# Low halves of a split-precision kernel's weights placed 64 bytes further in SBUF

## What is computed

```python
for l in range(DEPTH):                                   # DEPTH = 1
    x = x + 0.5 * swiglu(rms_norm(x, ffn1_norm[l]), ffn1_gate[l], ffn1_up[l], ffn1_down[l])
    x = x + hybrid_mixer(rms_norm(x, mix_norm[l]), w_in[l], ..., w_out[l], lam_init)
    x = x + 0.5 * swiglu(rms_norm(x, ffn2_norm[l]), ffn2_gate[l], ffn2_up[l], ffn2_down[l])
return rms_norm(x, final_norm)

def swiglu(h, w_gate, w_up, w_down):                     # D_FF = 2816
    return (jax.nn.silu(h @ w_gate) * (h @ w_up)) @ w_down
```

## The kernel before

| tiles | start modulo 256 |
|---|---|
| xg_hi, xg_lo, w_hi, w_lo, h_hi_s, h_hi_w, h_lo, mixed_hi, mixed_lo, first_hi, first_lo | 128 |
| s_hi, s_lo (behind `offset_of_s`, 192 bytes), raw_u, t_raw | 64 |
| sum_hi, sum_lo (behind `offset_of_sums`, 64 bytes), gate_s, snap, sq | 128 |
| x, raw, rinv, ones | 0 |

## Time and profile before

### The profile page before, as it was taken

One profiled execution on the slowest core, in us unless ns is written; L12 is line 12 of the kernel. 1 busy time (PEld: TensorE's weight loads), 2 busy tenths in 40 slices (PEclk: granted clock), 3 DMA queues, 4 the chain that ended last, 5 costly groups with the idle time before them and its releaser, 6 DMA issues. The chain is left out here.

```text
span 990.8 us, 16666 instructions
## 1 busy us (share of the span) xinstructions
PE 964.2 (97%) x6360; PEld 859.3 (87%) x6360; DVE 682.7 (69%) x945; ACT 438.7 (44%) x688; POOL 355.9 (36%) x232
## 2 busy tenths in 40 slices
PE   9999999999999999999989999999999999999996
PEld 8789999998888888777978788888999999888885
DVE  6599998997534364775756874459999998753344
ACT  7555455545422223555723233354555555543331
POOL 0767767670012151000102004377776767000002
PEclk9999999999999999999989999999999999999998
DMA  6323333322232244112211113233333232222222
GB/s 203 119 95 103 109 112 100 117 95 83 94 93 96 95 131 136 65 47 66 74 39 65 64 65 107 85 107 106 114 99 124 88 127 85 85 92 79 97 95 86
DMA packets 30638, 95.07 MB, mean 96 GB/s; under 512 B 4112, under 2 KB 7344, under 8 KB 30592
## 3 DMA queue, kind: packets, MB, share of 16 engines
q1 hardware_dynamic: 28400, 90.98, 28.4%
q0 software_dynamic: 896, 2.39, 0.9%
q10 hardware_dynamic: 1296, 1.07, 0.3%
HBM read 92.00 MB, written 2.42 MB: 95 GB/s over the span
## 5 line engine op out<-in xcount | busy, mean ns | idle before, releaser
L1376 DVE TENSOR_TENSOR w_lo<-raw,w_hi 128x1024 fp32r<-128x1024 f32 (+3 forms) x130 | 187.2, 1440 | 167.4 <-ACT w_hi L1002 167.3
L1002 ACT ACTIVATE w_hi<-raw 128x1024 fp32r<-128x1024 f32 (+3 forms) x130 | 134.2, 1032 | 208.8 <-PE ps L508 208.8
L506 PE MATMUL ps<-xg_hi,w_hi 128*128 128x256 f32 (+1 forms) x552 | 188.1, 341 | 4.1 <-DVE w_lo L1376 2.5
L508 PE MATMUL ps<-xg_hi,w_lo 128*128 128x256 f32 (+1 forms) x552 | 184.4, 334 | 0.0
L507 PE MATMUL ps<-xg_lo,w_hi 128*128 128x256 f32 (+1 forms) x552 | 184.2, 334 | 0.0
L506 PE MATMUL ps<-s_hi,sum_hi 128*128 128x256 f32 x576 | 159.8, 277 | 2.2 <-ACT snap L1095 2.1
L507 PE MATMUL ps<-s_lo,sum_hi 128*128 128x256 f32 x576 | 159.3, 277 | 0.0
L508 PE MATMUL ps<-s_hi,sum_lo 128*128 128x256 f32 x576 | 159.2, 276 | 0.0
L507 PE MATMUL ps<-h_lo,w_hi 128*128 128x512 f32 x330 | 128.4, 389 | 0.0
L506 PEld LDWEIGHTS ps<-xg_hi,w_hi 128*128 128x128 f32 x552 | 104.3, 189 | 24.1 <-issue 13.5
L508 PEld LDWEIGHTS ps<-xg_hi,w_lo 128*128 128x128 f32 x552 | 104.4, 189 | 10.9
(11 more groups left out here) (240 smaller groups left out, 1906.8 us busy)
## 6 DMA issues: line engine op xcount, KB each, us to landing
raw<-up_w SPq DMA_DIRECT2D x50, 512.0 KB, 4.2
raw<-down_w SPq DMA_DIRECT2D x38, 512.0 KB, 3.3
raw_u<-up_w SPq DMA_DIRECT2D x36, 512.0 KB, 3.4
raw<-t_w SPq DMA_DIRECT2D x18, 512.0 KB, 3.3
raw<-out_w SPq DMA_DIRECT2D x8, 512.0 KB, 3.3
raw<-nat_w SPq DMA_DIRECT2D x6, 576.0 KB, 3.9
x<-xT SPq DMA_DIRECT2D x8, 256.0 KB, 6.0
out<-x SPq DMA_DIRECT2D x8, 256.0 KB, 2.2
```

What stands on the lines that cost most here:

```text
L506: pe.matmul(out_ap, a[0], b[0], start=first, stop=False, skip_group_check=resumed)
L508: return pe.matmul(out_ap, a[1], b[0], start=False, stop=last, skip_group_check=resumed)
L1002: act.activation(dst, raw[:, slot(s), 0:w], ACT.Copy).then_inc(hi_ready, 1)
L1376: dve.tensor_tensor(lo, raw[:, slot(s), 0:w], hi, ALU.subtract).then_inc(lo_ready, 1)
```

## The change

Three unused tiles are added. One of 16 floats (64 bytes) ahead of `w_lo` moves it from 128 to 192 modulo 256, and one of 48 floats (192 bytes) behind it brings everything that follows back to its place modulo 256. One of 64 bytes ahead of `sum_lo` moves that from 128 to 192. No instruction, wait or transfer is added, removed or put elsewhere in the order.

```diff
@@ -162,7 +162,9 @@
         xg_hi = sb("xg_hi", [P, KT, S], F32R)
         xg_lo = sb("xg_lo", [P, KT, S], F32R)
         w_hi = sb("w_hi", [P, 2, SLOTW], F32R)
+        sb("below_w_lo", [P, 16])
         w_lo = sb("w_lo", [P, 2, SLOTW], F32R)
+        sb("above_w_lo", [P, 48])
 
 
         with ExitStack() as st:
@@ -174,6 +176,7 @@
             t_raw = sb("t_raw", [P, 3, HW], stack=st)
             sb("offset_of_sums", [P, 16], stack=st)
             sum_hi = sb("sum_hi", [P, 5, HW], F32R, stack=st)
+            sb("below_sum_lo", [P, 16], stack=st)
             sum_lo = sb("sum_lo", [P, 5, HW], F32R, stack=st)
             gate_s = sb("gate_s", [P, 2, S], stack=st)
             snap = sb("snap", [P, 3, HALF], stack=st)
```

## The result

The changed kernel takes 1004.04 us (median of 4 runs, 1003.03 to 1004.91) beside 993.21 us for the kernel before: a ratio of 1.0104, with a 95% interval of 1.0091 to 1.0117. It is slower by 1.0%, 10.8 us between the medians. The profiled span grew from 990.8 to 1003.0 us, by 12.2 us. One execution of the first kernel of experiment 7 (1589.72 us) and one of the kernel before beside it (1925.14 us) were slow and are left out of all medians and ratios.

A forecast was written before the change was run, and what follows sets the result against it. TensorE, busy 97% of the span, bounds the kernel by how closely matmuls follow. Gains of 4.4 + 2.9 = 7.3 us, less 0.8 us lost at waits, take 6.5 us off 992.66: 986.2 us; range 982.5 to 1001.5 us.

The forecast's parts named there:

- The constant belongs to the pair of addresses, not to the width.: TensorE matmuls: the remainder over the column rate, some 13 ns at distance 0, 6.6 ns for s, holds at every width.
- (a): 512-column matmuls with w_lo stationary: 658 steps go to distance 64, 6.7 ns less each, 4.4 us gained.
- A step depends on its own pair alone: Three-matmul products: only the step L507 to L508 gets a new distance and so a new time; 512 columns at 0.220 us.
- (b): 256 columns of xg under w_lo and sum_lo: 432 steps gain 6.7 ns each, 2.9 us.
- (c): sum_lo under s: 576 steps go from distance 64 to 128; bounds 3.8 us gain or loss, taken as nothing.
- (d): Token-major products: 96 steps stream w_lo under a load of xg_lo; bounds plus and minus 0.6 us, taken as nothing.
- (e): gate_s, snap and sq behind sum_lo move by 64 too; no cost, as VectorE has 8% in hand.
- (f): Everything behind w_lo moves by 256 bytes, none modulo 256, and no transfer changes in size: nothing.
- Broken locks: Rival, chance 0.28: after each jump TensorE's two streams never settle; 8.4 us more, 1001 us; 1009 us at full loss.
- Narrow only: Rival, chance 0.14: the 512-column step is already undisturbed, so its gain falls away; 2.9 us less, 990.1 us.
- Distance 128 collides: Rival, chance 0.10: sum_lo under s at distance 128 collides like 0, costing 3.8 us; 2.7 us less, 990.3 us.
- No effect: Rival, chance 0.12: addresses don't matter, s matmuls are faster for another reason; nothing moves, 992.9 us.

The follow-up runs named there:

- experiment 7: Against the kernel before: sum to 192, s to 128, w untouched, 1000.79 us; the same with unit slabs 16 floats further in their slots, 998.50 us.
- experiment 3: Against the kernel before: w and sum, both halves, at 192 and s at 128, so every loop has distance 64; 1006.38 us, ratio 1.0125.
- experiment 4: Against the kernel before, s kept at 64: w and sum, both halves, at 160, 192, 0, 64, 96; 1006.55, 1002.72, 1007.93, 1005.81, 1005.60 us, one run each.
- experiment 6: Against the kernel before: xg, w and mixed, both halves, all at 192; h, s and sum keep their places modulo 256; 1003.27 us, one run.
- sum_lo experiment: Against the kernel before: only sum_lo moved to 192, with gate_s, snap and sq kept at their places; 1000.49 us, ratio 1.0063.
- experiment 2: Against the changed kernel: every second call of `three` issues its matmuls in reverse order, same addresses; 1003.68 us, ratio 1.0095 to the kernel before.
- experiment 5: Against the kernel before: w_lo, xg_lo and mixed_lo at 192, 998.82 us, ratio 1.0044; xg_lo and mixed_lo alone at 192, 995.36 us.
- experiment 8: Against the kernel before: only the unit slabs moved within their slots, 64 bytes up, 992.28 us, ratio 0.9985; 192 bytes up, 991.92 us, ratio 0.9977.

## Why the prediction was wrong, step by step

- **What bounds the kernel, and where a change of places can act.** Right. The loss lies in TensorE's steps, and TensorE's idle time didn't grow.
- **"The constant belongs to the pair of addresses, not to the width."** This is the first step that failed. It rested on a remainder of 13 ns at 256, 384 and 512 columns at distance 0, and on one other distance, seen at 256 columns alone. The remainders are alike at distance 0 and part elsewhere: at 64 the wide steps have 233.3 ns (experiments 3, 4, 6) instead of the 220 forecast. (a) was to bring 4.4 us and cost 6.8 (3.9 + 2.0 + 0.9).
- **A step depends on its own pair alone.** This is the second. "of every three steps one, L507 to L508, gets a new distance" was taken to mean that only this one gets a new time. In the down product of the changed kernel that step has 229.3 ns on the mean (226.8 before), the one ahead of it 228.4 (226.7), and the one behind it, whose own pair is at distance 0 as before, 235.8 (227.0). Most of the loss at 512 columns lies in a step that the prediction left untouched.
- **(b), xg at 256 columns.** Right in its sign: 1.1 + 0.9 = 2.0 us instead of 2.9. Not in its way, and so near by luck: over w all three steps fell by 1 to 2 ns (120.2, 118.8 and 119.7 to 118.9, 117.6 and 118.3), not one by 6.7.
- **(c), sum_lo under s, taken as nothing.** This is the largest term that was off. It cost 7.5 us in steps, 6.5 with the pauses, against an upper bound of 3.8. That bound counted one step of three; the jump lengthened all three (to 119.4, 119.6 and 116.4 ns from the starts of L509, L510 and L511 to the next). With constant distances of 64, 64 and 128 the mean of three would be (2 x 113.3 + 119.1) / 3 = 115.2 ns, measured is 118.4. The wide ones are alike: (2 x 226.7 + 233.3) / 3 = 228.9, measured 231.1, so that one odd pair in three costs the double of its own price. So what a step costs can't be added up from constant distances.
- **(d), nothing:** the token-major step is 174.2 ns after 174.0. **(e), nothing:** the sum_lo experiment shows none that can be told from noise. **(f), nothing:** no run tests it alone.
- **Broken locks** came nearest in its numbers and its signs. It priced the wide steps at 0.230 (measured 0.231), s at 0.120 (0.118), narrow xg at 0.1175 (0.118), and the full loss at 1009 us; measured 1004.0. The reason that it gave, streams that never settle, isn't what the rows show: the wide steps do settle, on 228, 229 and 236 ns repeated from product to product; with half the jumps they are as long (experiment 2), and constant distances other than 0, without any jump, cost 229.7 to 233.4 ns (experiments 3 and 4). Its chance was too low for a poor reason: that a round trip between s and xg costs 20 ns and gives back 20 ns says what two changes cost a unit, and nothing of a change every one or two matmuls.
- **Narrow only** was right in one thing: 226.7 ns is the least that any wide product showed. It was wrong that wide steps don't depend on the pair.
- **Distance 128 collides** was near for s: 119.1 ns held constant, between 113.3 and 120.2.
- **No effect**, the reading of the Trainium skill (SBUF — State Buffer, SBUF: two separate sides), is excluded: only unused tiles were added, and the time moved by 1%. The section speaks of engine against engine. These runs show that a step of TensorE's gets up to 6.7 ns longer with the place of its weights against that of its moving tile, and the measurement decides. By the isolated gap that the Trainium skill gives (TensorE: Matmul & The Clock Gate, Back-to-back issue gap) the freed step is, by estimate, 215.8 ns at 512 columns; no kernel here came below a mean of 226.7.

What stays open. That the two reads disturb each other is what all runs agree with, but it is argued and not shown: no row shows a single read. No run leaves out the other engines' reads and writes of the moved tiles; against them as the cause stands that 228, 229 and 236 ns repeat with every product of three, whatever those engines do meanwhile. That the distance counts modulo 256 is an assumption too, with one row for it: in experiment 6 mixed and w moved apart by 256 bytes, and the step stayed at 226.7 ns. Neither the distance of each pair nor the number of jumps explains the wide step when one half is moved (experiments 2 and 5). One candidate is that a weight load overlaps more than one moving stream: in the changed kernel the loads last 188 ns in the profile, and the s steps 118. And it isn't known what selects between 113 and 118 ns at distance 64: the value can change at a wait for `snap` (experiments 3, 7 and 8), but not at each, a different product ahead seems to change it (experiment 6), and in the kernel before the s runs, entered from distance 0, are mostly at 113 (mean 114.1).

## What to carry to other kernels

Where TensorE is saturated with matmuls that each load new weights, read the step from start to start, apart for each width and each pair of tiles, and treat the start of a tile modulo 256 as a parameter that has to be measured: here a distance that helps 256 columns cost 6.6 ns a step at 512. Keep operands that follow each other (the high and the low half) at the same place; moving one of them lengthened all three steps of a product, at 512 columns most of all one that it doesn't touch. A pattern read at one width or from one settled stretch is a hypothesis, and a step that has two steady values can get longer by an edit elsewhere (s from 114.1 to 117.9 ns in experiment 6) or by one short wait.

## What the runs showed of the hardware

- float32r, 512 columns, a new weight load for each: 226.7 ns a step at distance 0, 229 to 230 at -64, 232.6 to 233.4 at 32, 64, 128 and -32 (experiments 3, 4 and 6).
- The same with the low weights alone at 64: 228, 229 and 236 ns in turn, 231.1 on the mean; the longest is the step whose own pair is at distance 0.
- 256 columns: 120 ns at distance 0; at 64 either 113.3 or about 117.8; 113.7 (xg over sum, experiment 6) and 118.0 (xg over w, w at 64) at -64; 117 to 119 at 32, 96, 128 and -32.
- Behind one wait of TensorE, even one that shows as a single step of 160 ns among steps of 113, the stream can go on at 118 with the same operands (experiments 3, 7 and 8), and stay there for the rest of a loop (3 and 7).
